# A hybrid decoder layer on one NeuronCore: two thirds of the projection by features run in units inside the gated recurrence

## What is computed

```
proj = h @ w_in      # q|k|v | zf | zi | zq | zg | za | zh
att  = merge of 3 dilated-window attentions over q, k, v                # 256 wide
f    = lb + (1 - lb) * sigmoid(zf);  S_t = diag(f_t) S_{t-1} + (1 - f_t) zi_t^T;  o_t = S_t^T zq_t
o_h  = rms_norm(o) * g * silu(zg)                                        # 4 heads, states of 128x128
mix  = (sigmoid(za) * (att @ w_att_branch) + sigmoid(zh) * (o_h @ w_hg_branch)) @ w_out
```

## Time and profile before

| | |
|---|---|
| median of three runs | 5438.93 us |
| the profiled execution | 5438.2 us |
| its span | 5436.5 us |
| TensorE busy | 4740.7 us, 87% |
| DVE busy | 2576.0 us, 47% |
| ACT busy | 1217.9 us, 22% |
| projection by features, first matmul to last evacuation | 542.4 to 810.9 us |
| recurrence, first load to last product of the samples' norm | 1276.2 to 1605.0 us |

### The profile page before, as it was taken

One profiled execution on the slowest core, in us unless ns is written; L12 is line 12 of the kernel. 1 busy time (PEld: TensorE's weight loads), 2 busy tenths in 40 slices (PEclk: granted clock), 3 DMA queues, 4 the chain that ended last, 5 costly groups with the idle time before them and its releaser, 6 DMA issues. The chain is left out here.

```text
span 5436.5 us, 72628 instructions
## 1 busy us (share of the span) xinstructions
PE 4740.7 (87%) x28529; PEld 2539.1 (47%) x28529; DVE 2576.0 (47%) x4545; ACT 1217.9 (22%) x1415; POOL 1035.2 (19%) x606
## 2 busy tenths in 40 slices
PE   7598997663767588999999996999999999999994
PEld 2354446432553354555555552444444444444441
DVE  4321004215754330699988953666565333333334
ACT  4200112212323110334343431000001111111113
POOL 1100000002210100000000004555555323232320
PEclk9799995575558799999999997999999999999997
DMA  6322211422115321389987775555555222222212
GB/s 239 125 79 76 103 65 59 117 63 79 45 51 200 108 86 65 125 198 217 227 206 163 159 154 138 144 145 145 145 145 140 72 70 71 68 76 65 70 48 76
DMA packets 1018959, 628.36 MB, mean 116 GB/s; under 512 B 855142, under 2 KB 921062, under 8 KB 1014795
## 3 DMA queue, kind: packets, MB, share of 16 engines
q1 hardware_dynamic: 447306, 503.26, 30.7%
q10 hardware_dynamic: 557600, 71.31, 8.7%
q0 software_dynamic: 13824, 50.51, 2.5%
HBM read 445.15 MB, written 210.54 MB: 121 GB/s over the span
## 5 line engine op out<-in xcount | busy, mean ns | idle before, releaser
L2409 PE MATMUL ex_psy<-ex_vhi,ex_wboth 128*128 128x512 f16 x4352 | 1327.4, 379 | 61.1 <-issue 52.7
L2409 PE MATMUL ex_psy<-ex_vlo,ex_wboth 128*128 128x512 f16 x2304 | 874.0, 379 | 0.0
L2067 POOL TENSOR_SCALAR ex_v<-ex_v 128x1024 f32<-128x1024 f32 x128 | 369.1, 2884 | 2231.3 <-DMA ex_v<-in_peer_v_dram 2231.3
L2409 PEld LDWEIGHTS ex_psy<-ex_vhi,ex_wboth 128*128 128x128 f16 x4352 | 426.1, 98 | 586.6 <-issue 54.9
L2368 PE MATMUL ex_psa<-h_hi,ex_uth 128*128 128x512 f16 (+1 forms) x3072 | 640.8, 317 | 9.0 <-ACT ex_wa L2096 9.0
L2368 PE MATMUL ex_psa<-h_lo,ex_uth 128*128 128x512 f16 (+1 forms) x3072 | 640.7, 317 | 0.0
L2368 PE MATMUL ex_psa<-h_hi,ex_utl 128*128 128x512 f16 (+1 forms) x3072 | 640.7, 317 | 0.0
L2336 DVE TENSOR_TENSOR ex_acc<-ex_acc,ex_psy 128x512 f32<-128x512 f32 x558 | 371.7, 683 | 456.9 <-PE ex_psy L2409 456.2
L2325 DVE SCALAR_TENSOR_TENSOR ex_wa<-ex_wa,ex_gate 128x1088 f32<-128x1088 f32 x128 | 177.6, 1387 | 469.0 <-ACT ex_wa L2096 429.4
L2409 PEld LDWEIGHTS ex_psy<-ex_vlo,ex_wboth 128*128 128x128 f16 x2304 | 225.6, 98 | 262.9 <-issue 0.8
L2368 PEld LDWEIGHTS ex_psa<-h_lo,ex_uth 128*128 128x128 f16 x3072 | 229.7, 98 | 242.9 <-issue 1.0
(11 more groups left out here) (332 smaller groups left out, 6510.8 us busy)
## 6 DMA issues: line engine op xcount, KB each, us to landing
gate_all<-rt_stage ACTq DMA_DIRECT2D x34, 2048.0 KB, 20.2
ex_gate<-gate_all SPq DMA_DIRECT2D x128, 544.0 KB, 6.6
ex_u<-in_peer_u_dram SPq DMA_DIRECT2D x128, 512.0 KB, 3.7
ex_v<-in_peer_v_dram SPq DMA_DIRECT2D x128, 512.0 KB
act_all<-ex_wa SPq DMA_DIRECT2D x80, 544.0 KB
ex_wa<-act_all SPq DMA_DIRECT2D x80, 544.0 KB, 5.0
adw<-in_ada_w_dram SPq DMA_DIRECT2D x12, 2048.0 KB
pn_w<-in_w_in_dram SPq DMA_DIRECT2D x8, 1664.0 KB, 7.0
```

The costliest lines, as they stand in the source:

```text
L2067: nc.gpsimd.tensor_scalar(v[:, :], v[:, :], SPLIT, None, ALU.mult).then_inc(v_sc, 1)
L2409: mm = nc.tensor.matmul(ps_y[n % YB][:, :], w, v_[:, a * 512:(a + 1) * 512], start=(j == 0), stop=(j == len(mms) - 1))
```

## The change

The 2048 columns of za and zh leave `project_features`, which keeps 1024 columns in chunks of 256 (two blocks). `h_hi` and `h_lo` stay in memory through the attention stages up to the recurrence, so these stages are now called inside `mixer`. In the recurrence, prompt tile n also makes chunk n of the gates, 256 features, in five units: unit 1 the 64 sample tokens of both blocks, units 0, 2, 3 and 4 a block's half of 512 prompt tokens. A unit fills one of two PSUM banks, which are taken from the four of the increments. TensorE's order in a tile is now: sums, unit 0, transposes, increments 0 and 1, unit 1, L1498, first half of unit 2, L1506, L1511 of chunk 0, increment 2, second half of unit 2, L1511 of chunk 1, increment 3, first half of unit 3, L1511 of chunk 2, second half of unit 3, L1511 of chunk 3, sum of squares, unit 4. ACT evacuates the units (`empty`) and makes the high weights; DVE makes the low weights at the end of a tile, for the next one; SP loads weights and stores gates. An increment waits for DVE's addition (`tmp_done`) and no more for its scaling. `inter` starts one higher, so DVE's product for a chunk waits for L1511 of the chunk two before. The tiles are written out, without a hardware loop. The diff, cut:

```diff
-def mixer_input(pr):
+def mixer(pr):
...
-        project_features(pr, "pt", h_hi, h_lo, w_v, C_ZQ, TRC, t["proj_t"], 0, 3 * P)
+        project_features(pr, "pt", h_hi, h_lo, w_v, C_ZQ, 2 * HW, t["proj_t"], 0, 2 * P)
+        for stage in (attention_prompt, attention_sample, attention_merge):
+            pr.clear_semaphores()
+            stage(pr)
+        pr.clear_semaphores()
+        recurrence(pr, h_hi, h_lo, w_v)
...
-def recurrence(pr):
+def recurrence(pr, h_hi, h_lo, w_v):
...
-        ps_u = [ps(f"ps_u{c}", [P, HH, HK]) for c in range(4)]
+        ps_u = [ps(f"ps_u{c}", [P, HH, HK]) for c in range(2)]
...
+        ps_z = [ps(f"ps_z{b}", [P, 512]) for b in range(2)]
+        w = [sb(f"w{s}", [P, KD, ZC]) for s in range(2)]
+        w_hi, w_lo = ([cx.enter_context(nc.sbuf_tensor(f"hg_{n}{s}", [P, KD, ZC], F16)) for s in range(2)] for n in ("whi", "wlo"))
+        z = [[sb(f"z{s}{j}", [P, TOK]) for j in range(2)] for s in range(2)]
...
-        def tiles(eng, tile, first):
-
-            with eng.Fori(0, PT // 2 - 1) as i:
-                for d in range(first, first + 2):
-                    tile(i * 2 + d, d % 2, P, CH, "p")
-            for n in range(PT - 2 + first, PT + 1):
+        def tiles(tile, first):
+            for n in range(first, PT + 1):
                 tile(n, n % 2, *((P, CH, "p") if n < PT else (NS, NT, "s")))
...
+            def load_weights(c, s):
+                sp.dma_start(w[s][:, :, :], w_v[:, :, C_ZA + c * ZC:C_ZA + (c + 1) * ZC]).then_inc(w_in[s], 16)
+
+            def store_gates(c, s):
+                sp.wait_ge(emptied, c * UNITS + UNITS + 2)
+                for j in range(2):
+                    row = 2 * HW + c * ZC + j * P
+                    sp.dma_start(t["proj_t"][row:row + P, :], z[s][j][:, :]).then_inc(z_stored[s], 16)
+
...
-                if not (isinstance(n, int) and n > PT - 2):
+                if n:
+                    store_gates(n - 1, 1 - s)
+                if n + 2 < PT:
+                    sp.wait_ge(w_lo_done, n + 1)
+                    load_weights(n + 2, s)
+                if n + 2 <= PT:
                     sp.wait_ge(squared, n + 1)
-                    load(n + 2, s, NS if isinstance(n, int) else P)
+                    load(n + 2, s, P if n + 2 < PT else NS)
...
             load(0, 0, P)
+            for c in range(2):
+                load_weights(c, c)
             load(1, 1, P)
...
+            def high(c):
+                act.wait_ge(w_in[c % 2], c // 2 * 16 + 16)
+                if c >= 2:
+                    act.wait_ge(filled, (c - 1) * UNITS)
+                nc.scalar.activation(w_hi[c % 2][:, :, :], w[c % 2][:, :, :], ACT.Copy, scale=SPLIT).then_inc(w_hi_done, 1)
+
...
+            def empty(c, u):
+                act.wait_ge(filled, c * UNITS + u + 1)
+                if u == 0 and c >= 2:
+                    act.wait_ge(z_stored[c % 2], c // 2 * 32)
+                bank = ps_z[(c * UNITS + u) % 2]
+                if u == 1:
+                    nc.scalar.activation(z[c % 2][0][:, SEQ:TOK], bank[:, 0:NS], ACT.Copy, scale=1.0 / SPLIT)
+                    out, src = z[c % 2][1][:, SEQ:TOK], bank[:, NS:2 * NS]
+                else:
+                    j, a = ((0, 0), None, (0, 512), (1, 0), (1, 512))[u]
+                    out, src = z[c % 2][j][:, a:a + 512], bank[:, :]
+                nc.scalar.activation(out, src, ACT.Copy, scale=1.0 / SPLIT).then_inc(emptied, 1)
...
                     exponentials(n + 1, 1 - s, after)
+                if n:
+                    empty(n - 1, 4)
                 act.wait_ge(k_tr, n + 1)
                 nc.scalar.copy(kt[:, :, r], ps_cn[:, :].rearrange("p (h t) -> p h t", h=HH)[:, :, r]).then_inc(k_t, 1)
                 if kind == "p":
+                    empty(n, 0)
                     logs(n + 1, after)
-                act.wait_ge(inter, n * 4 + nch + 1)
+                    empty(n, 1)
+                    if n + 1 < PT:
+                        high(n + 1)
+                    empty(n, 2)
+                    empty(n, 3)
+                act.wait_ge(inter, n * 4 + nch + 2)
...
+            act.sem_inc(emptied, 2)
             exponentials(0, 0, P)
             logs(0, P)
-            tiles(act, tile, 0)
+            high(0)
+            tiles(tile, 0)
...
+            def low(c):
+                dve.wait_ge(w_hi_done, c + 1)
+                nc.vector.scalar_tensor_tensor(w_lo[c % 2][:, :, :], w[c % 2][:, :, :], SPLIT, w_hi[c % 2][:, :, :],
+                                               ALU.mult, ALU.subtract).then_inc(w_lo_done, 1)
...
                 dve.sem_inc(tile_done, 1)
+                if n + 1 < PT:
+                    low(n + 1)
...
-            dve.sem_inc(inter, 1)
+            dve.sem_inc(inter, 2)
...
+            low(0)
...
+            def fill(c, u, ks):
+                if c >= PT:
+                    return
+                q, bank = c * UNITS + u, ps_z[(c * UNITS + u) % 2]
+                if ks[0] == 0:
+                    pe.wait_ge(w_lo_done, c + 1)
+                    pe.wait_ge(emptied, q + 1)
+                spans = [(0, SEQ, NS, 0), (1, SEQ, NS, NS)] if u == 1 else [(*((0, 0), None, (0, 512), (1, 0), (1, 512))[u], 512, 0)]
+                for j, a, width, at in spans:
+                    cols = slice(j * P, (j + 1) * P)
+                    for k in ks:
+                        for e, (y, x) in enumerate(((w_hi, h_hi), (w_hi, h_lo), (w_lo, h_hi))):
+                            mm = nc.tensor.matmul(bank[:, at:at + width], y[c % 2][:, k, cols], x[:, k, a:a + width],
+                                                  start=(k == 0 and e == 0), stop=(k == KD - 1 and e == 2))
+                if ks[-1] == KD - 1:
+                    mm.then_inc(filled, 1)
...
                 nc.tensor.matmul(ps_cn[r, :], tri[:, r], lf[r, :], start=True, stop=True).then_inc(sums, 1)
+                fill(n, 0, range(0, KD))
                 pe.wait_ge(k_done, n + 1)
...
-                increments(0)
+                for c in range(2):
+                    increments(c)
+                fill(n, 1, range(0, KD))
                 pe.wait_ge(k_t, n + 1)
...
                 mm.then_inc(a_done, 1)
-                for c in range(1, 4):
-                    increments(c)
+                fill(n, 2, range(0, 4))
                 pe.wait_ge(am_done, n + 1)
...
                     mm.then_inc(inter, 1)
-                    if c + 4 < nch:
-                        pe.wait_ge(s_done, n * 4 + c + 1)
-                        increments(c + 4)
+                    if c + 2 < nch:
+                        pe.wait_ge(tmp_done, n * 4 + c + 1)
+                        increments(c + 2)
+                    if c < 3:
+                        fill(n, (2, 3, 3)[c], range(4, 8) if c != 1 else range(0, 4))
...
                 pe.wait_ge(squared, n + 1)
...
                                  start=True, stop=True).then_inc(msum, 1)
-
-            tiles(pe, tile, 0)
+                fill(n, 4, range(0, KD))
...
-STAGES = (conditioning, mixer_input, attention_prompt, attention_sample, attention_merge, recurrence, mixer_merge,
-          mixer_output, peer)
+STAGES = (conditioning, mixer, mixer_merge, mixer_output, peer)
```

More of the change, by code:

```diff
@@ L1233, in recurrence @@
     fi_in, tmp_done = [pr.sem(f"hg_fi{s}") for s in range(2)], pr.sem("hg_tmp")
+    w_in, z_stored = ([pr.sem(f"hg_{n}{s}") for s in range(2)] for n in ("win", "zstored"))
+    w_hi_done, w_lo_done, filled, emptied = (pr.sem(f"hg_{n}") for n in ("whi", "wlo", "filled", "emptied"))
+    ZC, UNITS = 2 * P, 5
     with ExitStack() as cx:
@@ L1298, in _ @@
             sp.wait_ge(stored, (PT + 1) * 16)
+            for p in range(2):
+                sp.wait_ge(z_stored[p], PT // 2 * 32)
         @block.scalar
@@ L1324, in tile @@
                 nc.scalar.activation(em[:, :, 0:nch], ps_ct[:, :, rows:rows + nch], ACT.Exp).then_inc(exps, 1)
-                after = NS if isinstance(n, int) and n == PT - 1 else P
+                after = NS if n == PT - 1 else P
                 if kind == "p":
                     exponentials(n + 1, 1 - s, after)
+                if n:
+                    empty(n - 1, 4)
                 act.wait_ge(k_tr, n + 1)
@@ L1373, in _ @@
             prepare(0, 0, P, CH, "p")
-            tiles(pool, prepare, 1)
+            tiles(prepare, 1)
         @block.vector
@@ L1431, in tile @@
                     dve.wait_ge(u_done, q + 1)
[L1432 removed]
+                    nc.vector.tensor_tensor(s_in, sp_[c % 2][:, :, :], ps_u[c % 2][:, :, :], ALU.add).then_inc(tmp_done, 1)
                     dve.wait_ge(tmp_done, q + 1)
@@ L1463, in _ @@
             correct_log(0, P)
-            tiles(dve, tile, 0)
+            low(0)
+            tiles(tile, 0)
         @block.tensor
         def _(pe):
+            def fill(c, u, ks):
[14 more added lines that the diff above has]
+                    mm.then_inc(filled, 1)
             def tile(n, s, rows, ch, kind):
@@ L1490, in increments @@
```

(6 more changed lines are left out.)

1 line of the change is left out of this document (removed).

## The result

| | before | after |
|---|---|---|
| median | 5440.75 us (5434.79 to 5445.71, four runs) | 5313.79 us (5310.58 to 5317.89, four runs) |
| ratio | | 0.9767 [0.9753, 0.9782] |
| the profiled execution | 5438.2 us, span 5436.5 | 5310.58 us, span 5308.9 |

The direction and most of the accounting held; the recurrence grew by much less than forecast.

A forecast was written before the change was run, and what follows sets the result against it. TensorE alone was taken to bound the projection, and a chain at mostly 1.2 GHz the recurrence. The projection loses 180 us, the recurrence gains 97 (prompt tiles 32.5 to 45.0 us): net -83, 5355 us, range 5318 to 5415.

The forecast's parts named there:

- The projection: Projection by features: 16 of 24 blocks, shorter prologue and smaller first load take off 179.6 us, ends 178.6 and 181.
- Step 1: Prompt tile, sum of squares to unit 0: unit 0 waits for DVE's low weights until T+10.4, TensorE idle 3.3 us.
- Unit 0's clock fall: Each prompt tile: the idle 3.3 us before unit 0 drops the clock, 3.6 us at half rate, costing 1.8 us.
- Step 4: Prompt tile, unit 1: 48 matmuls of 64 columns at 57 ns each, 2.7 us; 1.3 and 5.5 kept as ends.
- from step 3 to step 5, thin work for 5 us: Prompt tile, transposes through L1506: a second clock fall per tile, costing 2.5 us, ends 0 and 6.
- Steps 2, 3, 5, 6 and 7: Prompt tile: unit 0 5.2; transposes, increments 2.5; L1498 1.0, half unit 2.6, L1506 1.0; chunk loop 13.6; finish 1.8 us.
- The gain is nil: Prompt tile's chunk loop: relaxing DVE's wait by one chunk gains nothing, as TensorE's queue takes over 3.4 us per chunk.
- Without them, up to 1 us twice: Chunk loop: two banks instead of four cost nothing with the units there, up to 1 us twice without them.
- (a): Rival, prompt tiles: the clock never falls, 40.8 us per tile, 5322 us; chance 0.17.
- (b): Rival, chunk loop: thin products pull the clock down; all low 5462 us, chance 0.04, half low 5409 us, chance 0.13.
- (c): Rival, prompt tiles: every burst starts and ends at low clock, tile 72.8 us, 5577 us; chance 0.05.
- (d): Rival, prompt tiles: evacuations or low weights hold the banks, 3 to 6 us more per tile, 5379 to 5403; chance 0.08.

The follow-up runs named there:

- experiment 6: The changed kernel with unit 4 cut to one of its 24 matmuls: 5329.89 us, ratio to the kernel before 0.9807.
- experiment 2: The changed kernel with DVE's low weights made before its normalising chain: 5273.19 us (again 5269.83 beside the changed kernel's 5303.52 on one chip).
- experiment 5: The changed kernel with unit 1's 48 matmuls of 64 columns issued three times: 5327.59 us, ratio to the kernel before 0.9804.
- experiment 11: The kernel of experiment 10 with 4 more unread matmuls behind each increment of the sample tile's loop: 5276.17 us, ratio to the kernel before 0.9701.
- experiment 3: The changed kernel with the old strict wait, DVE's product waiting for L1511 of the chunk before: 5315.88 us, ratio to the kernel before 0.9789.
- experiment 4: The kernel before the change, with the relaxed wait alone: 5411.11 us, ratio 0.9960.
- experiments 1: The changed kernel without the units, gates made in the old projection, two banks and relaxed waits kept: 5424.08 us, ratio to the kernel before 0.9983.
- experiment 7: The changed kernel with units 2 and 3 cut to one matmul each: 5256.05 us, ratio to the kernel before 0.9678.
- experiment 10: The kernel of experiment 2 with 12 unread 512-column matmuls between the sample tile's sums and transposes: 5264.83 us, ratio to the kernel before 0.9694.

## Why the prediction was right or wrong

**The projection** came out to the microsecond: 180.0 us against 179.6, with 3.0 us of it at the start, as the terms of the sum have it. The stretch "from about 529 to 635 us" under what would show it didn't follow from that sum, which gives 539.4 to 630; the matmuls ran from 539.4 to 629.7.

**Step 1, unit 0 waits for DVE's low weights**, was right in kind and size. T for the tile above is 1231.80 and unit 0 starts at 1242.25, T+10.45, where T+10.4 was forecast; the wait is 3.50 us for 3.3, and its releaser is L1461. That unit 4 is free is shown by experiment 6, and that this wait is what is late, by experiment 2.

**Unit 0's clock fall** was forecast at 1.8 us and costs 1.7 (39.0 and 40.7, 41.8 and 43.5). It was forecast for every tile and came in five of eight in the one profile and six in the other: about 5 us less.

**Step 4, unit 1, was mis-sized.** I took 57 ns per matmul, from the nearest row, twice as wide; it is 29 ns, the lower end. Experiment 5 gives the same 29 ns from a difference. The term was 2.7 us and is 1.41: 10 us over eight tiles. The choice of "nearest row" was wrong in its reasoning: the row's 57 ns per 128 columns and the group's 28 ns for 64 are the same time per column, and that the weights change with each matmul adds nothing that shows in either. The Trainium skill (TensorE: Matmul & The Clock Gate, section Back-to-back issue gap) puts a matmul of up to 64 columns at about 60 cycles, 25 ns; the trace has 29. The disagreement over the weight load that the prediction found is none of lengths: a load's record has a median of 98 ns, near the 107 that it quotes, but in unit 1 a matmul, each with its load, starts every 29 ns. The loads overlap, so their length is no pace:

```profile
L1543 PEld LDWEIGHTS hg_ps_z<-h_hi,hg_whi x384: 95/98/181, 1122.8 to 1437.9; 128*128 128x128 f16 x192
```

**The clock fall "from step 3 to step 5, thin work for 5 us", did not happen**, and this is the step of the prediction that failed. It was worth 2.5 us per tile, 20 us in all, half of the error. In neither profile of the changed kernel does the clock fall there, and with 4.2 us of thin work in place of 1.4 (experiment 5) it doesn't either. The fall in the conditioning stage that I had taken as precedent is behind f32 products of 9 rows and idle time, not behind f16 work that fills the queue. The stretch was also taken for longer than it is: transposes, increments and unit 1 run in 3.6 us. Why it held here stays open: in experiment 11 the clock fell behind 4.3 us of narrow f32 products with 0.51 us of waiting in them (1404.2 to 1408.5), and in a prompt tile no more than 2.9 us of such products stand in one piece (1256.27 to 1259.15); no run makes such a piece longer. The granted clock over the tiles was 0.97, where 0.85 to 0.9 was forecast.

**Steps 2, 3, 5, 6 and 7** held: 5.2 us for unit 0 plus the fall (1242.25 to 1249.12 is 6.9), 2.2 for the transposes and increments (2.5), 1.0, 2.6 and 0.9, 13.55 for the loop from 1257.16 on (13.6), and 1.8. At the full clock the sum was 40.8; less the 1.3 of unit 1 it is 39.5, and 39.0 was measured.

**The relaxed wait and the banks.** "The gain is nil" is near: 0.24 us per tile (experiment 3), while the same edit alone gives 24 us (experiment 4). "Without them, up to 1 us twice" fits the 1.7 per tile of experiments 1 and 4, which hold the new order as well.

**The sample tile** was given 2 us and gained 6.3, 4 us of the error. Of this the relaxed wait gives 3.3 in the kernel before (78.0 to 74.7), and 1.0 to 1.5 in the changed one; most of the rest is its sums and transposes, which now start at the full clock: the transposes begin 3.86 us behind the sums (1438.82 to 1442.68) instead of 7.41 (1559.45 to 1566.86).

**The rivals.** (a), the clock never falls, gave 5322 with unit 1 at 2.7 us, and 5312 with it at 1.4; it is the case nearest to what happened, five falls of 1.7 us apart. That the clock holds through the increments and unit 1 came true, and I gave it 0.17; that they "count as enough" by themselves is not shown, since dense work stands on both sides of them. (b), a fall in the loop, is no part of this kernel (0.97 and 1.00 in the windows), but it is real: without the half units the loop falls (experiment 7). (c) and (d) did not occur; no evacuation is waited for. Against (c) the prediction called up the projection's rows, but these hold a single wait, 23.26 us, behind which TensorE starts at 1.2 GHz, and no burst after it, so they say nothing against falls behind waits. Such falls are what the changed kernel has before unit 0, 3.4 us long each.

Together: unit 1 10 us, the fall that did not come 20, three falls fewer before unit 0 5, the rest of the tiles 4, the sample tile 4: 43 of the 44 us.

## What to carry to other kernels

Dense matmuls put between the steps of a latency-bound chain cost less than their own time, because they fill its waits and because they can lift the clock for the chain's own products (here 37 and some 80 of 177 us); price both, from rows at both levels. Then look at what the first of them waits for: one DVE operation placed before the chain instead of behind it was worth another 34 to 40 us, and taking away 5 us of matmuls per tile was worth nothing. For a short matmul without a row of its own, look for rows of two widths of the same type and see whether time goes by columns or by instructions: for f16 at 2.4 GHz it went by columns down to 64 (57 ns for 128, 29 for 64), for f32 it did not (eight products of 128, 32 and 8 columns have rows of 1.14, 0.98 and 1.06 us).

## What the hardware showed that I had not expected

- A matmul of 64 columns with weights of its own takes 29 ns in a run of 48 (1.41 us) and of 144 (4.2 us), although each loads 128 columns of weights and the record of a load is 98 ns long. The 64-column matmul behind two of 512 takes 28.
- The granted clock does not follow TensorE's busy time as the profile shows it. It stayed at 0.50 with 35.73 of 36.00 us busy, four 512-column f16 matmuls in every 20 included (experiment 11), fell in experiment 10 with TensorE busy 12.49 of the 13.00 us around the fall's beginning and 20.25 of the 20.50 after it, and was 0.99 over the prompt tiles of experiment 2, with f16 units and the same kind of f32 products between them.
- The low clock of 3.4 us appears behind a wait of 3.5 us, over the first matmuls that follow. It is not strictly repeated: of seven such waits five had the fall in one execution of the changed kernel and six in another, and four in experiment 5; of the waits of 3.7 us in experiment 3 all seven had it. In experiment 7 the three waits of 2.75 to 2.89 us before unit 0 had it as well, and the four of 1.4 to 1.6 us had none.
